# Adding the exp tiles of two key tiles on VectorE before the softmax denominator matmuls

## What is computed

```
def diff_attention(q, k, v, lam):
...
        s = jnp.einsum('bhqcd,bhkcd->bhcqk', qblk, k).astype(jnp.float32) * scale
        p = jax.nn.softmax(s, axis=-1)
        a = p[:, :, 0] - lam * p[:, :, 1]
        return jnp.einsum('bhqk,bhkd->bhqd', a.astype(v.dtype), v)
```

## Time and profile before

| What | Value |
|---|---|
| Time, median of 3 runs (lowest, highest) | 1084.35 us (1080.72, 1084.73) |
| Time of the profiled execution | 1084.59 us |
| Its span, slowest of 8 cores (core 2) | 1083.5 us; all cores 1068.6 to 1083.5 |
| PE matmul busy | 857.9 us, 79% |
| DVE busy | 526.8 us, 49% |
| ACT busy | 486.6 us, 45% |
| POOL busy | 145.4 us, 13% |

### The profile page before, as it was taken

The page is one execution under the profiler, slowest core; times in us unless marked ns, Lnnn a source line. Parts: engine busy times, 40 slices in busy tenths (PEclk is TensorE's granted clock), DMA queues, the critical chain, the costliest instruction groups (busy, mean ns, idle before and its releaser), DMA issues.

```text
span 1083.5 us, 12489 instructions; the slowest of 8 cores (1068.6 to 1083.5 us)
## 1 busy us (share of the span) xinstructions
PE 857.9 (79%) x4052; PEld 363.5 (34%) x4052; DVE 526.8 (49%) x745; ACT 486.6 (45%) x740; POOL 145.4 (13%) x272
## 2 busy tenths in 40 slices
PE   0135988777956588888888687789999899998988
PEld 0123333334522122222222234444444344443433
DVE  1033366545322314343343466546658756586568
ACT  3034557662115678888787623333430243302420
POOL 9400126100000000000000080302030130301000
PEclk9976999889977569999999888899999899999989
DMA  9995078801142000000000099502250440303004
GB/s 186 159 194 151 13 105 112 131 21 59 58 157 116 0 1 1 1 1 1 1 1 1 0 214 156 78 1 38 42 78 1 77 65 14 40 1 59 1 39 194
DMA packets 58175, 69.52 MB, mean 64 GB/s; under 512 B 8448, under 2 KB 48128, under 8 KB 57984
## 3 DMA queue, kind: packets, MB, share of 16 engines
q0 software_dynamic: 40896, 38.03, 24.9%
q1 hardware_dynamic: 17216, 30.70, 8.4%
HBM read 97.28 MB, written 9.44 MB: 98 GB/s over the span
## 4 chain that ended last, share of the span: by engine, by line
PE 58%; ACT 15%; DVE 10%; issue 7%; DMA 6%; POOL 2%; SPq 0%; ACTq 0%; DVEq 0%; POOLq 0%
PE ps_all L1012 9%; PE ps_all L1054 8%; PE ps_all L1005 7%; PE ps_all L964 4%; PE ps_all L777 4%; PE ps_all L794 4%; PE ps_all L472 3%; DMA arena<-w_ada 3%; ACT arena L783 3%; PE ps_all L797 3%; PE ps_all L796 2%; PE ps_all L795 2%; PE ps_all L401 2%; ACT arena L498 2%; PE ps_all L614 2%
## 5 line engine op out<-in xcount | busy, mean ns | idle before, releaser
L783 ACT ACTIVATE arena<-ps_all 128x1024 bf16<-128x1024 f32 (+1 forms) x168 | 155.9, 962 | 16.5 <-PE ps_all L778 16.5
L1012 PE MATMUL ps_all<-arena 128*128 128x512 bf16 x528 | 121.9, 389 | 10.6 <-DVE arena L1036 10.6
L1034 ACT ACTIVATE arena<-arena 128x1536 f32<-128x1536 f32 x22 | 32.6, 1483 | 200.7 <-DVE arena L1031 200.7
L1054 PE MATMUL ps_all<-arena 128*128 128x512 bf16 x528 | 118.0, 383 | 5.3 <-DVE arena L1036 5.3
L1005 PE MATMUL ps_all<-arena 128*128 128x512 bf16 x528 | 118.7, 381 | 0.0
L938 POOL DMA_DIRECT2D arena<-w_gate x48 | 25.6, 583 | 573.9 <-issue 429.3
L472 PE MATMUL ps_all<-arena 128*128 128x512 bf16 x336 | 82.3, 394 | 0.6 <-DVE arena L406 0.3
L777 PE MATMUL ps_all<-arena 64*128 64x512 bf16 (+1 forms) x168 | 64.7, 385 | 19.0 <-ACT arena L861 11.7
L1012 PEld LDWEIGHTS ps_all<-arena 128*128 128x128 bf16 x528 | 51.4, 100 | 80.4 <-issue 25.1
L401 PE MATMUL ps_all<-ident,arena 128*128 128x128 f32 x192 | 38.0, 351 | 48.7 <-DVE arena L394 45.4
L1054 PEld LDWEIGHTS ps_all<-arena 128*128 128x128 bf16 x528 | 50.6, 98 | 72.4 <-issue 16.0
(11 more groups left out here) (126 smaller groups left out, 1265.2 us busy)
## 6 DMA issues: line engine op xcount, KB each, us to landing
arena<-w_ada POOLq DMA_DIRECT2D x96, 128.0 KB, 10.8
arena<-xin SPq DMA_DIRECT2D x24, 512.0 KB, 8.8
yout<-arena SPq DMA_DIRECT2D x12, 512.0 KB, 2.7
arena<-w_down POOLq DMA_DIRECT2D x22, 256.0 KB, 8.6
arena<-w_in POOLq DMA_DIRECT2D x40, 128.0 KB, 28.3
arena<-w_gate POOLq DMA_DIRECT2D x40, 128.0 KB, 5.7
arena<-w_up POOLq DMA_DIRECT2D x40, 128.0 KB, 5.6
arena<-c_dfts SPq DMA_DIRECT2D x8, 512.0 KB, 9.8
```

The source lines that it names most:

```text
L783: S.op("act", lambda h: h.activation(out=Eo, in_=ps_all[:, pr[0] * 512: pr[0] * 512 + 1024].rearrange("p (c n) -> p c n", c=2)[:, :, 0:nq] ...
L1012: ins = h.matmul(bank(3 + b), wu_r[slot][:, k, fo:fo + 128], hT[:, k, b * 512:(b + 1) * 512], start=(k == 0), stop=(k == 7))
L1054: ins = h.matmul(bank(pb), uT[:, fl, i * 128:(i + 1) * 128], wd[:, fl, n * 512:(n + 1) * 512], start=(fl == 0), stop=(fl == nf - 1))
```

## The change

For every second key tile of a group, DVE adds the exp tiles of this unit and of the one before into one bf16 tile, `Esum`. The ones matmuls are issued in odd units only, and read `Esum`. In even units `sC` is the V matmuls alone. There is one buffer `Esum`, of 1024 columns (512 are used in prompt groups), in memory that was free in this stage. The add is issued at the start of `sC` of the odd unit, and the `S.op` of that unit's matmuls reads `Esum`.

```
+                odd = ti % 2 == 1
+                Eprev = E_r[(u - 1) % 3]
...
+                    zfirst = ti == 1
+                    if odd:
...
+                            S.op("dve", lambda h: h.tensor_tensor(out=Esum, in0=Eprev.rearrange("p c n -> p (c n)"),
+                                                                  in1=E.rearrange("p c n -> p (c n)"), op=ALU.add),
+                                 reads=[("E", erp), ("E", er)], writes=["Esum"])
                     def mm(h):
                         if nq == 256:
                             Ef = E.rearrange("p c n -> p (c n)")[:, 0:512]
-                            h.matmul(bank(bO), v_ap, Ef, start=first, stop=last)
-                            return h.matmul(bank(bZ), ones_bf, Ef, start=first, stop=last)
+                            ins = h.matmul(bank(bO), v_ap, Ef, start=first, stop=last)
+                            if odd:
+                                ins = h.matmul(bank(bZ), ones_bf, Esum[:, 0:512], start=zfirst, stop=last)
+                            return ins
                         h.matmul(OB(4), v_ap, E[:, 0, 0:nq], start=first, stop=last)
-                        h.matmul(OB(5), v_ap, E[:, 1, 0:nq], start=first, stop=last)
-                        h.matmul(OB(6), ones_bf, E[:, 0, 0:nq], start=first, stop=last)
-                        return h.matmul(OB(7), ones_bf, E[:, 1, 0:nq], start=first, stop=last)
-                    S.op("pe", mm, reads=[("E", er), "cbf"] + [kk for kk in kkeys if kk[0] in ("V", "Vc")],
+                        ins = h.matmul(OB(5), v_ap, E[:, 1, 0:nq], start=first, stop=last)
+                        if odd:
+                            h.matmul(OB(6), ones_bf, Esum[:, 0:512], start=zfirst, stop=last)
+                            ins = h.matmul(OB(7), ones_bf, Esum[:, 512:1024], start=zfirst, stop=last)
+                        return ins
+                    S.op("pe", mm, reads=[("E", er), "cbf"] + (["Esum"] if odd else []) + [kk for kk in kkeys if kk[0] in ("V", "Vc")],
                          writes=OZK)
```

More of the change, by code:

```diff
@@ L734, in build_nc @@
         osqP = [carve(oP + s_ * 512, [128, 256], BF16) for s_ in range(NPS)]; oP += NPS * 512
-        assert oP <= P23_END + 32768
+        assert oP <= P23_END + 19968
+        Esum = carve(P23_END + 19968, [128, 1024], BF16)
+        S.seed("Esum", ft)
         for s_ in range(NPS):
@@ L786, in sB, with sC @@
                         func=AF.Exp, scale=0.125), reads=[PB(pr[0]), PB(pr[1])], writes=[("E", er)])
-                def sC(v_ap=v_ap, E=E, er=er, first=first, last=last, kkeys=kkeys, u=u):
+                odd = ti % 2 == 1
+                Eprev = E_r[(u - 1) % 3]
+                erp = (u - 1) % 3
+                def sC(v_ap=v_ap, E=E, er=er, first=first, last=last, kkeys=kkeys, u=u, odd=odd, Eprev=Eprev, erp=erp, ti=ti):
+                    zfirst = ti == 1
+                    if odd:
+                        if nq == 256:
+                            S.op("dve", lambda h: h.tensor_tensor(out=Esum[:, 0:512], in0=Eprev.rearrange("p c n -> p (c n)")[:, 0:512],
+                                                                  in1=E.rearrange("p c n -> p (c n)")[:, 0:512], op=ALU.add),
+                                 reads=[("E", erp), ("E", er)], writes=["Esum"])
+                        else:
+                            S.op("dve", lambda h: h.tensor_tensor(out=Esum, in0=Eprev.rearrange("p c n -> p (c n)"),
+                                                                  in1=E.rearrange("p c n -> p (c n)"), op=ALU.add),
+                                 reads=[("E", erp), ("E", er)], writes=["Esum"])
                     def mm(h):
```

## The result

| What | Before | After |
|---|---|---|
| Median | 1083.32 us (10 runs) | 1166.8 us (8 runs) |
| Ratio, 95% interval | | 1.0771 (1.0756 to 1.0785) |
| Span of the profiled execution | 1083.5 us | 1165.6 us |

The forecast was 1162 us, in a range of 1124 to 1196.

The account below looks back on a forecast made before the run. PE sets the pace inside sample groups; at borders the new adds queue behind DVE's finishing work. 1084.6 + 47 (waits less saved matmuls) + 30 (clock falling) = 1162 us, range 1124 to 1196.

Parts of the forecast that it names:

- The add's price: One bf16 add of 1024 columns on DVE, taken as 0.70 us from a copy of the same width and type.
- The rival of 1.22 us: Each sample-group add costs 1.22 us and gets in each pair's way; about 1195 us with the clock; chance 0.06.
- N1's wait: Second of a sample group's units N0 to N11: PE waits for its add, queued behind DVE's border work; +4.6 us.
- N5's wait: Sixth unit of a sample group: its add queues on DVE behind the scaled output (L864), holding PE; +1.8 us.
- The group at full clock: A sample group takes 23.0 us instead of 18.6, +4.4 us, in 11 such groups.
- The clock: TensorE falls to 1.2 GHz at each sample-group border for 6 us, costing 2.7 us a group, +30 us in all.
- The rival without the fall: Sample-group borders leave PE waiting but the clock stays up: 1132 us, 1124 with a cheap add; chance 0.13.
- a clock that does not return in a group: PE stays at 1.2 GHz through sample groups: 1240 us at worst, 1192 with 12 us low; chance 0.14.
- The prompt groups: Prompt attention costs nothing more, its add and removed matmuls lying in PE's existing wait; bounds −3 to +8 us.
- If nothing waited: 31 us gained: Without waits, each of 72 even sample units saves 0.43 us of PE time, 31 us in all.
- rival "faster": The adds of N1 and N5 run when their exps end, so the pairs' saving remains: 1061 us; chance 0.04.
- the ring of three: Three exp tiles E: N3's exp waits for N1's add, but within PE's wait; claimed to cost nothing.

Follow-up runs that it names:

- Runs 2: Changed kernel, but the first pair of units of each sample group keeps its own ones matmuls, without an add; 1143.9 us, ratio 1.0558 to the kernel before.
- run 7: Changed kernel with adds only for the last three pairs of units of each sample group; 1079.1 us, ratio 0.9956 to the kernel before.
- run 6: Changed kernel with the first denominator's reciprocal made on ScalarE by Ln and Exp, DVE copying both numerators; 1143.1 us, ratio 1.054 to the kernel before.
- Run 5: Changed kernel with a sample group's scaled output issued on DVE behind the next group's third add, not ahead of it; 1148.8 us, ratio 1.0626.
- run 1: Changed kernel with score matmuls of three units repeated 5, 12 and 7 more times in each sample group but the first; 1142.1 us, ratio 1.0506.
- run 10: Kernel before with only the prompt groups changed, add and denominators complete; 1086.5 us, ratio 1.006.
- Run 3: Changed kernel without the adds; odd units' ones matmuls read their own exp tiles, even tiles left out of the denominators; 1073.4 us, ratio 0.988.
- Run 4: Kernel before, all ones matmuls kept, plus adds whose sums nobody reads; 1144.9 and 1147.1 us, beside 1086 for the kernel before.
- run 9: Changed kernel with adds only for each sample group's last four pairs, scaled output behind the first such add, prompt groups as before; 1078.1 us, ratio 0.9951.
- run 11: run 6 with score matmuls of three units repeated 5, 4 and 7 more times in each sample group but the first; 1102.3 us, ratio 1.0181.

## Why the prediction was right, step by step

- *The add's price:* 0.70 assumed, 0.689 measured; the copy was the right neighbour, and the two-per-cycle rule of the Trainium skill (VectorE: DVE Perf Modes, perf-mode tier table), with its estimate of 691 ns, agrees. The rival of 1.22 us is out.
- *N1's wait, +4.6 us:* 4.51. Runs 2 and 7 take away the add, run 6 the reciprocal, and the wait goes or shrinks to what was worked out: shown.
- *N5's wait, +1.8:* 1.78, and N9's 0.15 is 0.16. Run 5 takes 1.2 us of N5's wait away, worth 18 us with the clock's share.
- *The group at full clock, 23.0 us:* 23.06 in run 1.
- *The clock, +30 us:* 30 us over the groups and 25 to 28 in the kernel's time (run 1 against the change). That it falls in each group is read from the trace (0.70 to 0.86); that PE's gaps are the cause is shown by run 1, which changes only PE's work in the gaps. The "6 us" at 1.2 GHz a group was too small, 102/11 = 9.3 us, since the clock also fell behind the wait at N5. Part of that time was hidden in waits: in the group shown, 2.9 of 10.2 us at 0.50 lie in the wait at N1, where PE had nothing to do. The two errors cancel, so the mechanism of this term is shown, but that its size came out at 30 us is in part luck. The rival without the fall (1132) and that of a clock that does not return in a group (1192 to 1240) are out, though 9.3 us a group lies about midway between the 6 of the forecast and the 12 of the 1192.
- *The prompt groups, 0:* a little too low. The stage took 1.7 us longer (run 10), inside the bounds of −3 to +8. "Nothing" held for the groups behind the third, at 4.94 us; in the first three two adds stood uncovered and the clock fell earlier. Which of the two costs how much is open.
- *Two sums of the rivals* don't come out: 32 us a group gives 1084.6 + 11 × 13.4 = 1232, not 1240, and 1157 with the 30 us for the clock 1187, not 1195. The forecast's own sum does not use them; the upper end of the range, 1196, leans on them.
- *"If nothing waited: 31 us gained"* and the rival "faster" at 1061: wrong. Run 3 has no add and nothing waits for one, and it gains 13 us; at full clock its groups are 17.3 us apart, where PE alone would allow 16.0. That the exps set the pace there fits the rows and is not shown by a run. The forecast did not hang on it, since N5 to N11 was walked unit by unit.
- *Which path:* the prediction put the loss on PE's wait for Esum and called the exp's wait on the ring of three "nothing". Run 4 shows that the ring alone passes 60 us on, and that without any matmul taken away. In the change the two waits end together (522.20 on ScalarE, 522.25 on PE), so the sum did not feel it.

## What to carry to other kernels

Before work is moved onto an engine that looks idle on average, find where its instruction falls in that engine's program order, and what long instruction stands ahead of it just there: N1's and N5's adds, 23 of 72, cost 71 us of waits, the other 49 cost 3. Leaving out the first three adds of a group (run 7), or the first two with the output moved out of N5's way (run 9), made of a kernel 7.7% slower one 0.5% faster. Look, too, at what the freed engine waits for next, since that caps the gain (13 us here, not 31). And look at TensorE's clock: in run 6 all waits of PE for adds come to 36 us, and the fall of the clock cost 41 us over the groups (262.0 against 220.8 us in run 11).

## Hardware behaviour that was not expected

More matmuls made the kernel faster: 528 useless ones on a core saved 25 to 28 us (run 1), 352 saved about 40 us (run 11 against run 6). Short waits can keep the clock low as well as long ones: core 3 of run 6, with waits for adds of at most 1.8 us, had a mean granted clock of 0.79 over its groups, the change, with waits up to 4.5 us, 0.82. And cores that run the same program can settle in different patterns of the clock, 0.79 and 0.87, which made 17 us between core 3 and core 0 of run 6 (262.0 against 245.3 us).
